# A two-layer diffusion backbone in fp32: first layer's values split in high and low side by side, normalising on GpSimd, stage memory shared

## Chip, core and metric

One NeuronCore of a Trainium2 chip runs the whole program. The metric is the device time in microseconds of one launch. Kernel before: median 2120.17 us of 3 runs (2116.49 to 2120.89).

## The reference, cut

Tokens: 1024 latent ones on a 16 x 64 grid and 256 context ones, width 1024, fp32. Two layers, each: a modulation from a condition vector, one input projection to queries, keys, values and gate, a mixer, gating by SiLU, an output projection, a residual sum and a layer norm.

```python
h = x * (1.0 + sc) + sh
q, k, v, z = jnp.split(h @ w_in[l], 4, axis=-1)
# layer 0: 16 heads of 64, window of 8 x 16 grid cells plus all context keys, bias by relative position
s = jnp.concatenate([s_loc.reshape(b, h, GRID_W, n_win), s_ctx], axis=-1)
p = jax.nn.softmax(s, axis=-1)
y = p_loc @ v_win + p_ctx @ vc
# layer 1: 8 heads, difference of two softmax maps over all 1280 keys, rotary embedding, RMS norm per head
out = (y * jax.nn.silu(z)) @ w_out[l]
x_new = _layer_norm(DEEPNORM_ALPHA * x + (1.0 + g) * out, ln_g[l], ln_b[l])
```

Context queries of layer 0 attend to context keys alone. Layer 1 has no context output.

## The kernel before

The program is written engine by engine, in blocks: each engine has a queue of its own whose order is the order of the code, and semaphores tie the queues together. No planner reorders anything. A block ends when all engines have ended it. Blocks: `modulation` (layer 0's shift and scale, by matmul); `neighbourhood` (layer 0: tokens turned, modulated and split, then the chunks); `differential` (first `Project` of layer 0 and tokens of layer 1, then its chunks); `Project` of layer 1.

**Split products.** A fast matmul format (fp32r) holds fewer bits, so projections and scores split each operand in a high part (a rounding copy) and a low part (the difference), and sum the products. The projection does high x high, high x low, low x high (L528). Values (L1079) and transposes (L1065) are plain fp32.

**A chunk** is 128 of the 1024 columns: two heads of layer 0, or one of layer 1. `each_chunk` loops over 8, the last one written out apart. Within a chunk of layer 0: weight blocks come in the order value, key, query, gate, each for token groups of 512, 512 and 256 columns (12 products j). Four products of the next chunk (values, first keys) are pieces put between attention work (`fill`). `pe_part` turns the values by transposes (`turn_v`, L540), which open the chunk, then runs products 4 to 9.

**An item** is one head and one block of 128 queries: 16 local items (384 window keys + 256 context keys = 640 columns, five blocks of 128) and 4 context items (256 columns). Each goes: `scores` on TensorE (L1051 context, L1055 local, high and low keys), bias sum (L979) and negated row maximum (L981) on DVE, exponential with row sum on ScalarE (L933), reciprocal (L986) and normalising (L989) on DVE, transposes in batches of 3 and 2 blocks (L1065), a copy to SBUF on ScalarE (L940), value matmuls (L1079), gating straight from PSUM on DVE (L1002). Items are two apart in each queue. DVE also makes a quarter-row of layer 1's modulation per chunk (`LateModulation.sum`, L344), splits weights (`split_lo_part`, L497), and splits keys (`split_k`, L682, L686) and queries (`split_q`, L705, L709) from SBUF copies that ScalarE made (L582).

**Bias tables.** `Bias.expand` on GpSimd writes tables in DRAM: 32 DMAs from the table of relative positions (L270), a wait for all, 8 DMAs to a form by query (L277). `biases[0]` holds the first chunk's 2 heads and is expanded in the modulation block; `biases[1]` holds the other 14 and is expanded in the first layer's block, after the tokens are turned and a memset of the tables' frame in SBUF (L905). SP loads the tables of the next chunk with 48 DMAs in a chunk (L863), one head at a time; it waits for the expansion before the first of them, and weights and late rows queue behind it.

**Memory.** `Memory` holds arrays for the whole program; `big`, `aux`, `pt` and `extra_prob` are used by several stages for different things.

Of the kernel before, what the change touches and what calls it, by code (L numbers as in the profile page):

```python
# [19 lines left out]
P = 128  # L20
D = 1024
SEQ = 1024
# [47 lines left out]
CREDIT = 1  # L70
ROW_PAD = P
AHEAD = 4

# [6 lines left out]
class Memory:  # L80


    def __init__(self, nc, stack):
# [10 lines left out]
        self.v = sb("v", [P, TOK_TILES, P])  # L94
# [3 lines left out]
        self.big = sb("big", [P, 5120])  # L98
        self.aux = sb("aux", [P, 4608])
        self.extra_prob = sb("extra_prob", [P, TOK])  # L100
        self.pt = sb("pt", [P, 4, 4 * P])
# [20 lines left out]
def na_values(m, i):  # L122

    if i < 8:
        return m.big[:, 2560 + i * P:2560 + (i + 1) * P]
    return m.v[:, i - 8, :]


def na_values_from(m, i, n):

    first = na_values(m, i)
    return bass.AP(first.tensor, first.offset, [list(first.ap[0]), [1, n]])
# [8 lines left out]
def modulation(nc, m, stack, w_mod, cond_in, b_cols_in, lam_in, sub_in, ident_in, biases, load_tile, load_weights):  # L141
# [4 lines left out]
            [b[:, 0:D] for b in (m.k_raw, m.gate, m.y)] + [m.v[:, 0:KT, :].rearrange("p k n -> p (k n)")]  # L146
# [8 lines left out]
    row_buf = [m.pt[0:2, i, :] for i in range(4)]  # L155
    lam = m.extra_prob[:, 0:4 * HD]
    lam_prod = m.extra_prob[:, 4 * HD:5 * HD]
    sums = m.stats[:, 0:4]

    with nc.Block() as block:  # L160
        @block.sync
        def _(sp):
# [15 lines left out]
            sp.wait_ge(turned, 1)  # L178
# [69 lines left out]
class Bias:  # L248
# [14 lines left out]
    def expand(self, pool):  # L263
        n = len(self.heads)
        for rows in range(2):
            for cols in range(2):
                for c in range(STRIP):
                    src = self.rpb[rows, cols, self.heads[0], :, STRIP - 1 - c:2 * STRIP - 1 - c]
                    dst = self.by_column[rows, c, cols * NEAR:(cols + 1) * NEAR].rearrange("s h d j -> s (h d) j")
                    pool.dma_start(dst, bass.AP(src.tensor, src.offset, [[STRIP, NEAR], [RPB_W, n * RPB_H], [1, STRIP]]))\  # L270
                        .then_inc(self.columns_out, 16)
        pool.wait_ge(self.columns_out, 16 * 4 * STRIP)
        for rows in range(2):
            for r in range(BAND):
                src = self.by_column[rows, :, :, :, BAND - 1 - r:BAND - 1 - r + K_ROWS, :]
                dst = self.by_query[rows, r * STRIP:(r + 1) * STRIP]
                pool.dma_start(dst.rearrange("c s h n -> c (s h) n"), src.rearrange("c s h d j -> c (s h) (d j)"))\  # L277
# [6 lines left out]
def bias_parts():  # L284

    parts = []
    for b in range(ROW_BLOCKS):
        for half in range(2):
# [3 lines left out]
            for s in range(2):  # L292
                for kind in range(KINDS):
# [4 lines left out]
                    parts.append((half * 64 + s * CELL, b, at, high - low + 1, first - K_BAND0[b], last - first + 1,  # L298
                                  rows, cols * NEAR + low - strip + 1, first - band + 1))
# [3 lines left out]
class LateModulation:  # L303

    AHEAD = 3

    def __init__(self, nc, m, stack, w_mod, mod_rows):
# [1383 lines left out]
```

## Time and profile before

| | us |
|---|---|
| median of 3 runs | 2120.17 |
| the profiled execution | 2119.15 |
| its span | 2117.3 |
| TensorE busy | 1913.3 (90%) |
| VectorE busy | 1297.0 (61%) |
| ScalarE busy | 890.6 (42%) |
| GpSimd busy | 148.0 (7%) |
| granted TensorE clock, mean | 0.965 |

Busy time is the time in which an engine has an instruction under way; matmuls overlap each other, so a start-to-start distance says more of TensorE's cost than a duration does. A line number is that of the kernel before. In a row of a group, after the count stand the busy sum in us, the mean of one in ns, and the idle time before them with what ended it. In a row of the timeline the first two numbers are start and duration in us, and brackets hold the idle time before it and its releaser.

### The profile page before, as it was taken

How to read it: one execution, taken by the hardware profiler on the slowest of the kernel's cores; microseconds unless marked ns; L12 is line 12 of the kernel's file. 1: busy time of each engine (PE TensorE's matmuls, PEld its weight loads, DVE VectorE, ACT ScalarE, POOL GpSimd, SP SyncE). 2: the span in 40 equal slices, each digit the busy share in tenths (PEclk: the TensorE clock that was granted, in tenths of full speed). 3: DMA queues.
4: the chain of work that ended last, by engine and by line, in shares of the span. 5: the costliest groups of instructions: out<-in, count | busy, mean ns of one | idle time of the engine just before them, and what ended most of it. 6: DMA issues, size and time to landing. Idle time of an engine off the chain costs nothing. (4 is left out here: it accounts for less than half of the span.)

```text
span 2117.3 us, 31607 instructions
## 1 busy us (share of the span) xinstructions
PE 1913.3 (90%) x11121; PEld 1629.3 (77%) x11121; DVE 1297.0 (61%) x2074; ACT 890.6 (42%) x1560; POOL 148.0 (7%) x155
## 2 busy tenths in 40 slices
PE   6879799999999999968989999999999989998697
PEld 2768687978888888856867878787887878787576
DVE  1557384747474757585875566565747474747567
ACT  0434253535354444451134536463636363635410
POOL 4234000000000000001100000000000000000000
PEclk9899899999999999998999999999999999999899
DMA  8476422222222222125411010101000000001142
GB/s 272 67 59 49 110 62 55 62 54 64 58 61 56 63 54 65 44 91 179 149 70 40 11 40 10 40 10 38 12 30 20 30 20 23 16 20 40 55 175 100
DMA packets 137392, 130.80 MB, mean 62 GB/s; under 512 B 46672, under 2 KB 112560, under 8 KB 137216
## 3 DMA queue, kind: packets, MB, share of 16 engines
q1 hardware_dynamic: 125008, 98.22, 16.3%
q0 software_dynamic: 9744, 22.51, 6.0%
q10 hardware_dynamic: 2592, 9.44, 1.1%
q8 instruction: 29, 0.48, 0.1%
q14 instruction: 19, 0.16, 0.0%
HBM read 110.81 MB, written 22.00 MB: 63 GB/s over the span
## 5 line engine op out<-in xcount | busy, mean ns | idle before, releaser
L528 PE MATMUL acc<-h_hi,w_hi 128*128 128x512 f32 (+1 forms) x1408 | 524.7, 373 | 14.6 <-DVE w_lo L497 5.0
L528 PE MATMUL acc<-h_lo,w_hi 128*128 128x512 f32 (+1 forms) x1408 | 512.4, 364 | 0.0
L528 PE MATMUL acc<-h_hi,w_lo 128*128 128x512 f32 (+1 forms) x1408 | 512.3, 364 | 0.0
L528 PEld LDWEIGHTS acc<-h_hi,w_hi 128*128 128x128 f32 x1408 | 269.4, 191 | 55.6 <-issue 15.8
L528 PEld LDWEIGHTS acc<-h_hi,w_lo 128*128 128x128 f32 x1408 | 268.6, 191 | 42.4
L528 PEld LDWEIGHTS acc<-h_lo,w_hi 128*128 128x128 f32 x1408 | 269.6, 191 | 33.6
L1367 PE MATMUL acc<-k_dup,q_stack 128*128 128x512 f32 (+1 forms) x768 | 192.3, 393 | 38.2 <-DVE q_stack L709 24.5
L1281 DVE TENSOR_REDUCE stats<-acc 128x1 f32<-128x1280 f32 x128 | 190.3, 1487 | 53.0 <-PE acc L1367 52.9
L940 ACT ACTIVATE pt<-acc 128x256 f32<-128x256 f32 (+1 forms) x288 | 123.4, 432 | 203.5 <-PE acc L1065 203.3
L1367 PEld LDWEIGHTS acc<-k_dup,q_stack 128*128 128x128 f32 x768 | 145.9, 205 | 79.6 <-issue 24.4
L1388 PE MATMUL acc<-pt,v 128*128 128x128 f32 x1280 | 175.0, 277 | 0.8
L1220 ACT ACTIVATE pt<-acc 128x512 f32<-128x512 f32 (+1 forms) x192 | 100.8, 525 | 155.4 <-PE acc L1376 152.6
L1388 PEld LDWEIGHTS acc<-pt,v 128*128 128x128 f32 x1280 | 160.6, 193 | 3.0 <-issue 1.9
L1079 PE MATMUL acc<-pt,v 128*128 128x128 f32 x1024 | 159.4, 276 | 0.6 <-DVE y L1002 0.6
L1213 ACT ACTIVATE big<-acc,stats 128x1280 f32<-128x1280 f32 x96 | 127.5, 1329 | 76.0 <-DVE stats L1281 74.2
L1065 PE MATMUL acc<-ident,big 128*128 128x128 f32 x704 | 125.5, 277 | 35.5 <-DVE big L989 35.5
L1079 PEld LDWEIGHTS acc<-pt,v 128*128 128x128 f32 x1024 | 136.9, 192 | 2.5 <-issue 1.9
L1065 PEld LDWEIGHTS acc<-ident,big 128*128 128x128 f32 x704 | 85.8, 141 | 58.5 <-issue 23.0
L497 DVE TENSOR_TENSOR w_lo<-w_raw,w_hi 128x1024 fp32r<-128x1024 f32 x64 | 78.4, 1224 | 80.9 <-ACT w_hi L492 79.7
L933 ACT ACTIVATE big<-acc,stats 128x640 f32<-128x640 f32 (+1 forms) x160 | 116.5, 728 | 26.1 <-DVE stats L981 26.0
L1376 PE MATMUL acc<-ident,big 128*128 128x128 f32 x640 | 103.9, 277 | 24.0 <-DVE big L1294 23.4
L1574 PE MATMUL acc<-h_hi,w_hi 128*128 128x512 f32 x288 | 91.8, 400 | 25.5 <-DVE w_lo L1514 25.4
(189 smaller groups left out, 2725.1 us busy)
## 6 DMA issues: line engine op xcount, KB each, us to landing
w_raw<-in_w_in SPq DMA_DIRECT2D x64, 512.0 KB, 4.1
extra_prob<-in_w_mod SPq DMA_DIRECT2D x40, 256.0 KB, 2.8
w_raw<-y_t POOLq DMA_DIRECT2D x18, 512.0 KB, 5.6
w_raw<-in_w_out SPq DMA_DIRECT2D x16, 512.0 KB, 3.3
big<-in_w_mod SPq DMA_DIRECT2D x24, 256.0 KB, 2.8
y_t<-y SPq DMA_DIRECT2D x8, 640.0 KB, 3.4
y_t<-y SPq DMA_DIRECT2D x8, 512.0 KB, 2.8
big<-x POOLq DMA_DIRECT2D x8, 512.0 KB, 3.7
```

The source lines that it names most:

```text
L528: mm = nc.tensor.matmul(m.bank(self.bank_of(j), w), wt[:, b % 2, k, :], ht[:, k, t0:t0 + w], start=(k == 0 and i == 0), stop=(k == KT - 1 ...
L933: nc.scalar.activation(prob[:, i % PB, 0:it.width], all_scores(i), ACT.Exp, bias=stat(i, 2), accum_out=stat(i, 3)).then_inc(exp_done, 1)
L940: nc.scalar.activation(m.pt[:, n % 3, 0:w], m.bank(4 + n % 2, w), ACT.Copy).then_inc(pt_ready, 1)
L1065: mm = nc.tensor.transpose(m.psum[:, 4 + n % 2, t * P:(t + 1) * P], prob[:, i % PB, (a + t) * P:(a + t + 1) * P], m.ident[:, :])
L1079: mm = nc.tensor.matmul(m.psum[:, 6, (it.n % 4) * P:(it.n % 4 + 1) * P], na_values(m, it.blocks[a + t]), m.pt[:, n % 3, t * P:(t + 1) * P] ...
L1213: nc.scalar.activation(prob(mp, t), m.banks(3 * mp, 0, TOK), ACT.Exp, bias=stat(t, mp), accum_out=stat(t, 2 + mp)).then_inc(exp_done, 1)
L1220: nc.scalar.activation(m.pt[:, n % 4, 0:w], m.bank(6, w), ACT.Copy).then_inc(pt_ready, 1)
L1281: nc.vector.reduce_max(stat(t, mp), m.banks(3 * mp, 0, TOK), AX, negate=True).then_inc(max_done, 1)
L1367: mm = nc.tensor.matmul(m.bank(3 * mp + g, w), m.q_stack[:, mp, t * P:(t + 1) * P], m.k_dup[:, mp, part, k0:k0 + w], start=(part == 0), st ...
L1376: mm = nc.tensor.transpose(m.psum[:, 6, i * P:(i + 1) * P], prob(0, t)[:, (a + i) * P:(a + i + 1) * P], m.ident[:, :])
L1388: mm = nc.tensor.matmul(m.psum[:, 7, (t % 4) * P:(t % 4 + 1) * P], m.v[:, a + i, :], m.pt[:, n % 4, i * P:(i + 1) * P], start=(a + i == 0) ...
L1574: mm = nc.tensor.matmul(m.bank(2 * (i % 3) + half), yt[:, i % 2, k, :], wt[:, k, half * 512:half * 512 + 512], start=(k == 0 and n == 0), ...
```

## The change

Layer 0's attention is rewritten, layer 1's only renamed; arrays are placed stage by stage at shared addresses.

- Items go in pairs, a `Unit`: one head, two blocks of queries (both row blocks of a column block). 10 units in a chunk. TensorE's queue has a unit's scores, then the transposes of the unit before in batches of 3, 4 and 3 blocks (context: 4), value matmuls two batches behind, and products of the next chunk at two places of a step.
- Values are kept split, high and low side by side: 64 + 64 columns as one stationary operand, with 256 queries moving. ScalarE writes the high half of the turned probabilities (`take_hi`), DVE the low half (`take_lo`). The result has two halves, summed by `take_low` (ScalarE) and `sum_y` (DVE), then `gate_y`.
- Keys and queries are split straight from PSUM (`split_x_hi` on ScalarE, `split_x_lo` on DVE).
- Normalising goes to GpSimd, as a multiply with a factor of step 0; `biases[1]` is expanded ahead of it in the same queue, without waiting for the tokens. The memset of the tables' frame goes to the modulation block.
- Tables are loaded by kind of column block (3 kinds, 16 DMAs each). Late rows have two slots in place of three.
- The scratch for GpSimd's DMA descriptors is set to 4096 bytes. The call before named no size (the library's default is 16384).

```diff
-    def expand(self, pool):
+    def expand_columns(self, engine):
...
+    def expand_queries(self, engine):
+        engine.wait_ge(self.columns_out, 16 * 4 * STRIP)
...
             def _(pool):
...
-            biases[0].expand(pool)
+            biases[0].expand_columns(pool)
+            biases[0].expand_queries(pool)
+            nc.gpsimd.memset(near.bias[:, :], NEG).then_inc(near.bias_set, 1)
...
+class Unit:
...
+            self.batches = [(1, 0, [(0, 1), (1, 0), (0, 0)], [band(1), band(0)]),
+                            (2, 0, [(0, 2), (1, 1), (0, 3), (1, 3)], [band(2), ctx[0]]),
+                            (0, P, [(1, 2), (0, 4), (1, 4)], [band(3), ctx[1]])]
+        else:
+            self.width = CTX
+            self.batches = [(2, 0, [(0, 0), (1, 0), (0, 1), (1, 1)], ctx)]
...
             @block.gpsimd
             def _(pool):
-                pool.wait_ge(tokens.turned, 3 * KT)
-                nc.gpsimd.memset(m.aux[:, :], NEG).then_inc(bias_set, 1)
-                biases[1].expand(pool)
+                biases[1].expand_columns(pool)
+                biases[1].expand_queries(pool)
+
+                def chunk(c, last):
+                    def normalise(i):
+                        pool.wait_ge(recip_done, CREDIT + c * NI + (i + 1))
+                        factor = stat(i, 4)
+                        factor = bass.AP(factor.tensor, factor.offset, [list(factor.ap[0]), [0, units[i // 2].width]])
+                        nc.gpsimd.tensor_tensor(probs(i), probs(i), factor, ALU.mult).then_inc(p_ready, 1)
...
+                    p.act_part(act, c, lambda e: e.wait_ge(y_ready, CREDIT + c * COLS), last)
+                    for step in range(NU + 1):
+                        old = of_unit[step - 1] if step else []
+                        for n in old[:1]:
+                            take_hi(n)
+                        if step < NU:
+                            exp(2 * step)
+                        for n in old[1:2]:
+                            take_hi(n)
+                        if step % 2 and step >= 3:
+                            take_low(step // 2 - 1)
+                        if step < NU:
+                            exp(2 * step + 1)
+                        for n in old[2:]:
+                            take_hi(n)
...
+                        if step < NU:
+                            row_max(2 * step)
+                        for n in old[:1]:
+                            take_lo(n)
+                        if step < NU:
+                            row_max(2 * step + 1)
+                        for n in old[1:2]:
+                            take_lo(n)
+                        if step < NU:
+                            reciprocal(2 * step)
+                        if step % 2 and step >= 3:
+                            sum_y(step // 2 - 1)
+                        if step < NU:
+                            reciprocal(2 * step + 1)
+                        for n in old[2:]:
+                            take_lo(n)
+                        if step % 2 and step >= 3:
+                            gate_y(step // 2 - 1)
...
+                    def turn(n):
+                        s, j, slot, first, tiles, blocks = batches[n]
+                        pe.wait_ge(p_ready, CREDIT + c * NI + 2 * s + 2)
...
+                        for t, block in enumerate(blocks):
+                            for pt in (near.pt_hi, near.pt_lo):
+                                mm = nc.tensor.matmul(m.psum[:, 6, u.head * 2 * P:(u.head + 1) * 2 * P],
+                                                      near.values[:, block, u.head, :], pt[:, slot, t * 2 * P:(t + 1) * 2 * P],
...
+                    for step in range(NU + 1):
+                        if step < NU:
+                            scores(step)
+                        for position, n in enumerate(of_unit[step - 1] if step else []):
+                            turn(n)
+                            if n >= 2 and step < NU:
+                                values(n - 2)
+                            if step == NU - 1:
+                                values(n - 1)
+                            if position == 1:
+                                fill_in(step, MIDDLE)
...
-    nc = bacc.Bacc("TRN2", target_bir_lowering=False, num_devices=1)
+    nc = bacc.Bacc("TRN2", target_bir_lowering=False, num_devices=1, dynamic_dma_scratch_size=4096)
```

## Rows read from the trace of the kernel before

**Rows 1.** The page's first part: busy us, share of the span, instructions.
```profile
PE 1913.3 (90%) x11121; PEld 1629.3 (77%) x11121; DVE 1297.0 (61%) x2074; ACT 890.6 (42%) x1560; POOL 148.0 (7%) x155
```
**Rows 2.** Timeline of TensorE: the first transposes of chunks 0, 1, 2, 4, 5, 7.
```profile
93.27 1.03 PE L540 MATMUL acc<-ident,k_raw 128*128 128x128 f32 x8
...
212.99 1.03 PE L540 MATMUL acc<-ident,k_raw 128*128 128x128 f32 x8
...
329.25 1.03 PE L540 MATMUL acc<-ident,k_raw 128*128 128x128 f32 x8
...
537.32 1.03 PE L540 MATMUL acc<-ident,k_raw 128*128 128x128 f32 x8
...
641.37 1.04 PE L540 MATMUL acc<-ident,k_raw 128*128 128x128 f32 x8
...
849.48 1.03 PE L540 MATMUL acc<-ident,k_raw 128*128 128x128 f32 x8
```
**Rows 3.** Windows of chunk 4: projection, then attention; busy us (instructions), clock, DMA.
```profile
537.32:566.85 29.53, 29.53 (x163) 25.60 (x162) 12.15 (x18) 11.15 (x15) 0.00 (x0) 1.00 0.21 60
566.85:641.37 74.52, 70.56 (x485) 62.83 (x485) 53.01 (x104) 36.07 (x86) 0.00 (x0) 1.00 0.23 59
```
**Rows 4.** Timeline of GpSimd, 0 to 220 us.
```profile
6.87 20.72 POOL L270 DMA_DIRECT2D first_by_column<-in_rpb  x32
...
78.00 3.94 POOL L905 MEMSET aux<- 128x4608 f32 x1 [40.24 <-PE acc L397]
81.88 5.61 POOL L270 DMA_DIRECT2D rest_by_column<-in_rpb  x4
97.62 5.58 POOL L270 DMA_DIRECT2D rest_by_column<-in_rpb  x4 [10.14 <-issue]
...
206.41 5.28 POOL L277 DMA_DIRECT2D rest_by_query<-rest_by_column  x8 [10.27 <-DMA rest_by_column<-in_rpb]
```
**Rows 5.** Timeline of TensorE in chunk 4: projection of 256 columns, values.
```profile
558.98 0.28 PE L528 MATMUL acc<-h_lo,w_hi 128*128 128x256 f32 x1
559.10 0.28 PE L528 MATMUL acc<-h_hi,w_lo 128*128 128x256 f32 x1
...
585.58 0.61 PE L1079 MATMUL acc<-pt,big 128*128 128x128 f32 x4
```
**Rows 6.** Groups by line with shapes kept apart, whole span.
```profile
L1079 PE MATMUL acc<-pt,v 128*128 128x128 f32 x1024 | 159.4, 276 | 0.6 <-DVE y L1002 0.6
...
L1079 PE MATMUL acc<-pt,big 128*128 128x128 f32 x384 | 64.2, 276 | 0.4 <-DVE y L1002 0.3
...
L709 DVE TENSOR_TENSOR q_stack<-y,q_stack 64x512 fp32r<-64x512 f32 x64 | 43.9, 686 | 2.0
...
L671 POOL TENSOR_TENSOR big<-big,aux 128x512 f32<-128x512 f32 x32 | 41.4, 1293 | 820.4 <-DVE big L660 820.4
```
**Rows 7.** Timeline of chunk 4's attention, 611 to 613 us.
```profile
611.21 0.55 DVE L989 TENSOR_SCALAR big<-big,stats 128x640 f32<-128x640 f32 x1
...
611.89 0.54 PE L1065 MATMUL acc<-ident,big 128*128 128x128 f32 x3 [1.44 <-DVE big L989]
612.01 0.55 DVE L979 TENSOR_TENSOR acc<-acc,aux 128x384 f32<-128x384 f32 x1
...
612.47 0.49 ACT L940 ACTIVATE pt<-acc 128x384 f32<-128x384 f32 x1 [1.85 <-PE acc L1065]
612.60 0.82 DVE L981 TENSOR_REDUCE stats<-acc 128x1 f32<-128x640 f32 x1
```
**Rows 8.** Timeline of SP: the last chunk's result is stored.
```profile
949.37 0.35 SPq L889 DMA_DIRECT2D y_t<-y  x1
```
**Rows 9.** L270 issues at 81.9, at 84.7 and 86.1, at 112.2: time to landing.
```profile
DMA to landing us min/median/max: 8.0/8.0/8.0
...
DMA to landing us min/median/max: 10.2/10.7/11.2
...
DMA to landing us min/median/max: 5.8/5.8/5.8
```

More of the change, by code:

```diff
@@ L70 @@
 CREDIT = 1
+AHEAD = 4
 ROW_PAD = P
-AHEAD = 4
 def f(ap):
@@ L806, in neighbourhood @@
-    late = LateModulation(nc, m, stack, w_mod, mod_rows)
+    turned, pt_hi, pt_ready, av_done = sem("turned"), sem("pt_hi"), sem("pt_ready"), sem("av_done")
+    y_low, y_sum, y_ready, y_stored = sem("y_low"), sem("y_sum"), sem("y_ready"), sem("y_stored")
+    late = LateModulation(nc, m, near, stack, w_mod, mod_rows)
     counters += late.counters
-    items = [Item(h, n) for h in range(2) for n in range(TOK_TILES)]
-    NI = len(items)
-    NL = sum(it.local for it in items)
-    WMAX = LOCAL + CTX
@@ L823, in neighbourhood @@
-    NT = len(turns)
-    YG = 6
-    last_item = [max(i for i, it in enumerate(items) if it.y_group == g) for g in range(YG)]
-    local_before = [sum(x.local for x in items[:i]) for i in range(NI + 1)]
-    BL = 16 * 2 * len(bias_parts())
-    assert NI % 2 == 0 and NT % 6 == 0 and NI % PB == 0
-    z0, z1, z2 = p.gate_groups
-    fill = {-1: (0, z1, 0, 4), 0: (0, z1, 4, 8), 2: (0, z2, 0, 4), 3: (0, z2, 4, 8)}
-    for i, k in ((4, 0), (5, 2), (6, 4), (7, 6), (8, 7)):
-        fill[i] = (1, 0, k, min(k + 2, 7) if i < 8 else 8)
@@ L834, in neighbourhood @@
-    for i in range(4):
-        fill[9 + i] = (1, 1, 2 * i, 2 * i + 2)
-        fill[13 + i] = (1, 2, 2 * i, 2 * i + 2)
-        fill[17 + i] = (1, 3, 2 * i, 2 * i + 2)
-    filled = {i: (next_chunk, j) for i, (next_chunk, j, k0, k1) in fill.items() if k1 == KT}
+    units = [Unit(s) for s in range(2 * (COL_BLOCKS + 1))]
+    NU = len(units)
+    NI = 2 * NU
+    NL = sum(2 * u.local for u in units)
+    bias = near.bias[:, :].rearrange("p (h b s n) -> p h b s n", h=2, b=ROW_BLOCKS, s=KINDS * K_STRIPS)
@@ new lines, in bias_of @@
+    def bias_of(u, row):
+        s0 = u.kind * K_STRIPS
+        return bias[:, u.head, row, s0:s0 + K_STRIPS, :].rearrange("p s (g n) -> p g s n", n=CELL)
+    batches = [(s, j) + b for s, u in enumerate(units) for j, b in enumerate(u.batches)]
+    NT = len(batches)
+    of_unit = [[n for n, b in enumerate(batches) if b[0] == s] for s in range(NU)]
+    slot_free = [max([i + 1 for i in range(n) if batches[i][2] == b[2]], default=0) for n, b in enumerate(batches)]
+    local_before = [2 * sum(x.local for x in units[:i // 2]) + i % 2 for i in range(NI)]
@@ L840, in stat @@
+    filled = {step: piece[0:2] for (step, half), piece in fill.items() if piece[3] == KT}
     def stat(i, col):
@@ L892, in _ @@
+                sp.wait_ge(tokens.turned, 3 * KT)
                 for u in range(late.AHEAD):
                     late.load(sp, 0, u)
[L894 to L897 removed]
                 each_chunk(sp, chunk)
@@ new lines, in chunk @@
+                    for step in range(NU + 1):
[12 more added lines that the diff above has]
+                            take_hi(n)
+                        take_filled(step)
+                        if step == 3 and not last:
@@ L1123, in _, with differential @@
+                    if last:
+                        pe.wait_ge(p.gate_done, CREDIT + c * p.q_groups + 3)
+                    else:
+                        pe.wait_ge(p.evac, CREDIT + (c + 1) * p.evacs + 3)
+                    values(NT - 2)
+                    late.reduce(pe, c)
+                    values(NT - 1)
                 each_chunk(pe, chunk)
     return counters, run
-def differential(nc, m, stack, p, tokens, before, out_w, rope_in, y_out):
+def differential(nc, m, far, stack, p, tokens, before, out_w, rope_in, y_out):
```

854 lines of the change are left out of this document (462 added, 392 removed).

## The prediction

> **What bounds the kernel now.** I read the page first: TensorE is busy 90% of the span and no other engine more than 61% [rows 1]. So TensorE's queue is followed next, by stage. The program has a short start (modulation, then tokens), eight chunks of layer one, a join, eight chunks of layer two and an end; the change touches the first two. The transposes that open a chunk (turn_v, L540) date the chunks: chunk 0 begins at 93.27, then 212.99, 329.25, and so on at 537.32, 641.37 and, for the last, 849.48 [rows 2]. A steady chunk takes 641.37 - 537.32 = 104.05 us; chunk 0 took 119.7, chunk 1 116.3, together 27.9 above two steady ones. The table by stage splits a steady chunk in 29.5 us of projection, in which TensorE never rests, and 74.5 of attention, with 70.56 busy and 3.96 idle [rows 3]. GpSimd does nothing in either. Layer one is bound by TensorE's work, and what lies on GpSimd is free. In chunks 0 and 1 it isn't: GpSimd's queue there works on the bias tables until about 212 [rows 4], and the excess of 27.9 us hangs on DMA and on tables that come late.
>
> **TensorE's part.** Value matmuls in plain fp32 cost two instructions each: four in a row from 585.58 fill 0.61 us where one lasts 0.275, so they start (0.61 - 0.275) / 3 = 0.112 us apart [rows 5, 6]. The groups count (1024 + 384) / 8 = 176 in a chunk, 19.7 us [rows 6]. The new form joins two query blocks: a local unit (two items) has 6 value blocks x high and low = 12 matmuls of 256 columns, a context unit 4, so 8 x 12 + 2 x 4 = 104. Split projection matmuls of 256 columns follow each other by 559.10 - 558.98 = 0.12 us [rows 5], so 12.5 us. That takes 7.2 us from each chunk, 58 us in all, if TensorE stays the bound. The 88 transposes and the scores stay as many.
>
> **The splits.** Keys and queries are split straight from PSUM. DVE's 12.15 us of the projection stage [rows 3] are this splitting, but for one weight split of 1.2: about 10.7 us go, and 8 subtractions of 64x512 (0.69 us [rows 6]) and 4 of half the width (0.42 by proportion and a fixed part) come, 7.2. It gains 10 subtractions for low values (0.42 or less, 3.9), the low halves of turned probabilities (0.55 for 384 columns, priced by the sum of that width [rows 7], 0.69 for 512; 15.9 in all) and 2.7 in the new sum and gating, and loses 16 x 0.55 + 1.4 = 10.2 of normalising [rows 7]. That is 65 + 9 = 74 us in a chunk: no bound as a sum. In the projection stage ScalarE and DVE have 11 and 12 us of 29.5 [rows 3]; DVE gets 11 more and five sums of the late modulation (1.4 each), so it fills 25 to 29 of 29.5. I cost it at nothing; the cover is TensorE's 29.5 us. The duplication of the keys lies under the last two products too.
>
> **Normalising on GpSimd.** One item has 640 columns; GpSimd's multiply of 512 took 1.292 us [rows 6], so 1.6 us (1.4 to 1.8; a stride-0 factor may cost or save), where DVE took 0.55 [rows 7]. By itself hidden, it now lies in a chain, since the order written out makes each step need the one before. In step s TensorE turns unit s-1, whose two items must both be normalised. From that turn: ScalarE's copy begins 0.52 to 0.58 later (611.89 to 612.47) and takes 0.49, the low half 0.55, then the second row maximum (bias sum 0.59 from 612.01 to 612.60, maximum 0.82) [rows 7]: 2.5 to 3.1 us, I take 3.05. From there DVE still subtracts the second batch (0.69) and takes the first reciprocal (0.19) before GpSimd may start: GpSimd is then behind both, 2 x 1.61 in a row, and TensorE starts 0.13 after it [rows 6, 7] (the turn at 611.89 after the normalising from 611.21 to 611.76). With some 0.1 of handing over: 3.05 + 0.69 + 0.19 + 3.22 + 0.25 = 7.4 us a step. TensorE's own work in steps 2 to 5 is scores 1.19, transposes 1.08, values 1.44 and pieces of the next projection 2.72 = 6.4 us. So the chain, not TensorE, sets the steps.
>
> The attention stage, from its start: first turn at 8.0 (gating of the first group 1.65, two maxima 2.8, reciprocal, two multiplies), second at 16.1 (a gating pushes in), five steps of 7.4 to 53.1, 0.3 for the weight split in step 3, one more to 60.8, then two short context steps (5.7, 4.5) and 3.5 for the last values and the reduction of the late row: 74.5 us. That is the present 74.5 [rows 3]. The 7.2 us saved turn into waiting: a steady chunk stays at 104 (between 97, TensorE alone, and 109). The last chunk has no products of a next one as filler, so it was at 99.9 us to its store (949.37, [rows 8]) against 104.05 + 1.5 of a steady one; the chain makes it 106 to 109: +8 us.
>
> A rule that speaks against the change stands in the Trainium skill, SBUF — State Buffer, "Who interferes with whom": a DVE instruction with two SBUF inputs and a GpSimd instruction that reads SBUF exclude each other, the later one waits to the end. No row before shows both at once. It is rival (4) below, which is priced without it.
>
> **GpSimd's queue at the start.** This decides the sign. The tables of the other 14 heads are expanded by 32 + 8 DMAs on GpSimd; before they end it can't normalise anything. In the kernel before they start at 81.88 and the last eight at 206.41 + 5.28 [rows 4]: 130 us that hid behind nothing but SP's wait. After the change the wait for the tokens is gone, so they start at the block's start, 48 us; TensorE wants the first normalised unit at about 130 to 137.
>
> Their pace changes too. They come four at a time (5.6 us), then a pause until the fourth has landed: issue 86.1 + 11.2 = 97.3, next at 97.62 [rows 4, 9]. The first tables, with a seventh of the data, went 32 in a row with no pause, 20.72 us [rows 4]. So what is limited is not the number of DMAs but of pieces: by the code 630 runs in one large DMA, 90 in a small one; 2880 pass, 5 x 630 = 3150 don't. The change sets the descriptor memory to 4096 bytes where the library's default is 16384: a quarter, 720 to 787 runs, one large DMA at a time. The first of a burst lands 5.8 us (in the second listed) to 8.0 after its issue [rows 9]; I take 6.15 and 0.3 to the next, 32 x 6.45 = 206 us, bounded by 130 (no effect of the size) and 266 (8.0 each). The last eight: 5.3 of issue, two pauses: 12.5.
>
> The same limit splits the first tables in five bursts, four pauses of 5.4 minus some overlap; the queue ends the modulation stage with a memset of 3.9 us [rows 4] at about 61 instead of before the others are done (48): +13 (0 to 20). Addresses shared between stages add no wait of their own: the blocks' ends already order the stages, and late rows, which now wait for the tokens to be turned, are first summed in chunk 0, behind its 29.5 us of projection.
>
> **The sum.** Expansion ends 61 + 206 + 12.5 = 279.5; two multiplies and a turn: 283. Attention after the first turn 66.5: chunk 1 starts at 349.5, chunk 2 at 453.5 with no excess left, since tables and weights are now early. It was at 329.25 [rows 2]: +124. Chunks 2 to 6: 0. Last chunk: +8. Join and layer two: 0, their products and order are the same, and the second x tile is only fetched earlier beside TensorE. The profiled execution took 2119.15 us, span 2117.3, 1.0 below the median of 2120.17. 2119 + 124 + 8 = 2251; I say 2250.
>
> **Rivals.** (1) The size of the descriptor memory does nothing. Expansion runs 48 to 178, first turn 181.5, chunk 2 at 350.5: +21, with the last chunk +8: 2148. For it: the pause may have another cause; against it: small and large DMAs differ just by pieces. (2) Other side: besides (1), the chain is shorter than TensorE's work (multiplies below 1.2 us, or handed over earlier), chunks of 97: chunk 2 at 339, six times -7, last chunk +2: 2119 + 10 - 35 + 2 = 2096, faster. It decides once a step's chain is below 6.4 us and the tables end before about 190. For it: 7.2 us less TensorE work is sure; against: reciprocal after second maximum is written into the order. (3) Two large DMAs fit at once, 4.4 us each: 140 us, 2185. (4) GpSimd's multiply, 28 us of a chunk now, and DVE hold each other up in memory, or the landings take 8.0 each: four DVE pieces a chunk, each late by up to one multiply of 1.6 us on the chain, are 3 to 5 us, 24 to 40 in all, or 60 more at the start: 2280 to 2310. No row before has both engines on SBUF at once, so nothing speaks for or against it but that the pieces stand in the chain. (5) The new pieces do not overlap as written (projection stage runs over by DVE): +1 to 3 us a chunk, 2265.
>
> **Chances.** The forecast together with (5) 0.50, (4) 0.13, (3) 0.08, (1) 0.16, (2) 0.11, something else faster 0.02. The predicted time is the likeliest case, 2250. Leaving out (2) and the top of (4), the range is 2130 to 2290. Some 0.2% (4 us) is what a measurement tells from no change: faster 0.13, same 0.02, slower 0.85.
>
> **What would show it.** Right: GpSimd's row is full from 61 to about 280 with one table DMA every 6 to 7 us; TensorE idles some 140 us in chunk 0, released by GpSimd's multiply; L540's successors lie 104 us apart; TensorE's busy sum falls by about 55. In a step, the turn waits for the second multiply. Wrong: bursts of four as before (then 2150), TensorE without waits in steps 2 to 5 (then chunks of 97), multiplies far from 1.6 us, a second layer that moves by more than 3 us.

## The result, and the profile after

| | median of the runs, us | runs, us | profiled span, us | ratio, 95% interval |
|---|---|---|---|---|
| before | 2118.33 | 2111.96 to 2120.89 | 2117.3 | |
| after | 2214.97 | 2212.61 to 2218.07 | 2210.8 | 1.046, 1.043 to 1.049 |

The change makes the kernel 4.6% slower, 97 us. The forecast was 2250, with a range of 2130 to 2290.

The first part of the page of after answers to [rows 1]; busy us, share of the span, instructions:

```profile
PE 1857.1 (84%) x10545; PEld 1573.4 (71%) x10545; DVE 1375.2 (62%) x2246; ACT 935.6 (42%) x1648; POOL 325.9 (15%) x315
```

TensorE's work fell by 1913.3 - 1857.1 = 56.2 us, as the wider value matmuls promise, and yet its share fell from 90% to 84%: it waits more than it did. Where, the starts of the chunks tell, as in [rows 2] (timeline of TensorE, chunks 0, 2, 4 and 8 of sixteen; the last line is SyncE's store of the last result of layer one, as in [rows 8]; x8 and x2 only say how many transposes a line lumps together):

```profile
102.76 1.03 PE L534 MATMUL acc<-ident,k_raw 128*128 128x128 f32 x8
...
431.89 0.38 PE L534 MATMUL acc<-ident,k_raw 128*128 128x128 f32 x2
...
634.53 1.03 PE L534 MATMUL acc<-ident,k_raw 128*128 128x128 f32 x8
...
1216.78 1.03 PE L534 MATMUL acc<-ident,k_raw 128*128 128x128 f32 x8
...
1047.59 0.35 SPq L1028 DMA_DIRECT2D y_t<-y  x1
```

Chunk 2 starts 431.89 - 329.25 = 102.6 us later than before. From there a chunk takes 101.32 us where it took 104.05, so chunk 7 starts at 938.46, and five chunks have given back 13.7. The last chunk takes 1047.59 - 938.46 = 109.1 to its store instead of 99.9: +9.2. The join is 1.1 longer, layer two 5.8 shorter. The sum: 102.6 - 13.7 + 9.2 + 1.1 - 5.8 = 93.4, and the spans differ by 93.5.

GpSimd's timeline says where the 102.6 come from, answering to [rows 4], and TensorE's first turn of normalised probabilities stands behind it:

```profile
61.52 1.42 POOL L313 DMA_DIRECT2D rest_by_column<-in_rpb  x1 [1.55 <-POOLq L201]
67.36 1.43 POOL L313 DMA_DIRECT2D rest_by_column<-in_rpb  x1 [4.43 <-issue]
...
247.96 1.40 POOL L313 DMA_DIRECT2D rest_by_column<-in_rpb  x1 [4.38 <-issue]
253.72 3.34 POOL L322 DMA_DIRECT2D rest_by_query<-rest_by_column  x5 [4.36 <-DMA rest_by_column<-in_rpb]
...
263.53 2.47 POOL L1053 TENSOR_TENSOR near_prob<-near_prob,stats 128x640 f32<-128x640 f32 x2
266.05 1.33 PE L1246 MATMUL acc<-ident,near_prob 128*128 128x128 f32 x5 [125.74 <-POOL near_prob L1053]
```

The 32 large table DMAs go one at a time, (247.96 - 61.52) / 31 = 6.0 us apart (5.76 where nothing disturbs them), and the first multiply of chunk 0 stands behind all of them. TensorE waits 125.74 us in one piece. Its granted clock is at its lower level, 0.50, from 143.7 to 270.0 us, so chunk 0 pays a little for that too, in the first 4 us after the wait.

Inside a steady chunk, the windows of chunk 4 (projection, attention) answer to [rows 3], and the list of what TensorE waited for in it follows (us in total, times, longest):

```profile
634.53:664.50 29.97, 29.97 (x167) 26.07 (x166) 21.55 (x38) 17.43 (x31) 0.00 (x0) 1.00 0.34 100
664.50:735.85 71.35, 63.80 (x412) 55.72 (x411) 54.08 (x104) 35.35 (x82) 22.24 (x20) 1.00 0.18 45
```
```profile
PE acc L1261 <- DVE y L1166: 3.5, 3, 1.6
PE acc L1246 <- POOL near_prob L1053: 3.5, 4, 0.9
PE acc L1246 <- DVE near_pt_lo L1158: 0.4, 1, 0.4
```

The projection stage is still TensorE's alone: VectorE's 21.55 us lie under its 29.97. In the attention stage TensorE has 6.8 us less to do than in [rows 3], and it idles 7.55 where it idled 3.96. Half of that is the multiplies' chain (L1053). The other half was in nobody's sum: values (L1261) wait for VectorE's sum_y (L1166), which frees the bank of the result (the part of PSUM that holds it) for the next column.

### The profile page after: what moved, and what is told of

It is laid out like the page before. It is cut to its first block and busy times, and to the rows that moved or that the text cites. A ratio compares the mean times of both kernels' runs of the same rounds, so it can differ in the third digit from the quotient of the medians.

```text
span 2210.8 us, 30825 instructions
## 1 busy us (share of the span) xinstructions
PE 1857.1 (84%) x10545; PEld 1573.4 (71%) x10545; DVE 1375.2 (62%) x2246; ACT 935.6 (42%) x1648; POOL 325.9 (15%) x315
## 5 line engine op out<-in xcount | busy, mean ns | idle before, releaser
L1053 POOL TENSOR_TENSOR near_prob<-near_prob,stats 128x640 f32<-128x640 f32 (+1 forms) x160 | 177.9, 1131 | 597.7 <-DVE stats L1154 597.6
L1246 PE MATMUL acc<-ident,near_prob 128*128 128x128 f32 x704 | 116.0, 283 | 164.1 <-POOL near_prob L1053 157.9
L1158 DVE TENSOR_TENSOR near_pt_lo<-acc,near_pt_hi 128x384 fp32r<-128x384 f32 (+1 forms) x208 | 125.6, 604 | 175.6 <-ACT near_pt_hi L1092 174.4
L1092 ACT ACTIVATE near_pt_hi<-acc 128x384 fp32r<-128x384 f32 (+1 forms) x208 | 109.7, 528 | 273.5 <-PE acc L1246 231.8
L1392 ACT ACTIVATE far_prob<-acc,stats 128x1280 f32<-128x1280 f32 x128 | 169.9, 1328 | 72.2 <-DVE stats L1460 69.6
L1568 PE MATMUL acc<-far_pt,far_v 128*128 128x128 f32 x1280 | 175.6, 278 | 0.6
L1568 PEld LDWEIGHTS acc<-far_pt,far_v 128*128 128x128 f32 x1280 | 161.2, 194 | 3.2 <-issue 2.1
L1261 PE MATMUL acc<-near_pt_hi,near_values 128*128 128x256 f32 x416 | 126.9, 327 | 31.3 <-DVE y L1166 31.3
L1086 ACT ACTIVATE near_prob<-acc,stats 128x640 f32<-128x640 f32 (+1 forms) x160 | 116.8, 730 | 70.1 <-DVE stats L1150 60.7
L1555 PE MATMUL acc<-ident,far_prob 128*128 128x128 f32 x640 | 104.3, 278 | 25.7 <-DVE far_prob L1473 23.9
```

What stands on the lines that cost most here:

```text
L1053: nc.gpsimd.tensor_tensor(probs(i), probs(i), factor, ALU.mult).then_inc(p_ready, 1)
L1086: nc.scalar.activation(probs(i), all_scores(i), ACT.Exp, bias=stat(i, 2), accum_out=stat(i, 3))\
L1092: nc.scalar.activation(turned_part(near.pt_hi, n), turned_bank(n), ACT.Copy).then_inc(pt_hi, 1)
L1158: nc.vector.tensor_tensor(turned_part(near.pt_lo, n), turned_bank(n), f(turned_part(near.pt_hi, n)), ALU.subtract).then_inc(pt_ready, 1)
L1246: mm = nc.tensor.transpose(m.psum[:, 4 + n % 2, first + t * P:first + (t + 1) * P], probs(2 * s + row)[:, a * P:(a + 1) * P], m.ident[:, :])
L1261: mm = nc.tensor.matmul(m.psum[:, 6, u.head * 2 * P:(u.head + 1) * 2 * P], near.values[:, block, u.head, :], pt[:, slot, t * 2 * P:(t + 1) ...
```

## The experiments

Each ran beside the kernel before; medians are given, and chunk lengths come from the traces. The numbers of a trace belong to one execution, whose total can lie some us from the median.

**1. The descriptor memory alone.** In the kernel before, `Bacc(..., num_devices=1)` becomes:

```diff
-    nc = bacc.Bacc("TRN2", target_bir_lowering=False, num_devices=1)
+    nc = bacc.Bacc("TRN2", target_bir_lowering=False, num_devices=1, dynamic_dma_scratch_size=4096)
```

> The kernel before with one number changed: 4096 bytes of descriptor memory instead of the default. Theory (the size sets how many pieces may be under way): the 32 large table DMAs of the other heads go one at a time, 5.8 to 6.5 us apart, instead of four in 11.2 us; the first 32 small ones get pauses; the tables end at about 280 instead of 212, so chunk 1's attention (its place is 242 us) waits some 40 us more for them, and the run is 40 to 65 us longer: about 2170. Steady chunks stay at 104.05. Rival (the size does nothing, the pace after comes from something else in the change): bursts of four as before, 2118 within 4 us.

Measured 2199.9 against 2118.1: ratio 1.039 (1.036 to 1.041), 82 us for one number. GpSimd's timeline of this run:

```profile
17.61 5.18 POOL L270 DMA_DIRECT2D first_by_column<-in_rpb  x8 [5.49 <-issue]
...
105.18 1.41 POOL L270 DMA_DIRECT2D rest_by_column<-in_rpb  x1 [4.40 <-issue]
...
277.10 1.40 POOL L270 DMA_DIRECT2D rest_by_column<-in_rpb  x1 [4.34 <-issue]
282.83 3.33 POOL L277 DMA_DIRECT2D rest_by_query<-rest_by_column  x5 [4.33 <-DMA rest_by_column<-in_rpb]
```

A run is here one contiguous stretch of elements that a DMA moves, the prediction's piece. Small tables go in bursts of eight (8 x 90 runs = 720), large ones (630 runs) one at a time: it is the number of runs under way that is limited, and the limit follows the size. Chunk 0 took 104.0 us, chunk 1 203.5. The loss is larger than the 40 to 65 I gave, since I let only the bias loads wait. SyncE's wait for the tables also stands ahead of a weight load of the next projection, and TensorE waited 84.8 us for that (L497), in chunk 1. Steady chunks stayed at 104.1. The reverse, the changed kernel with the default size, was not run: its arrays leave no room in SBUF for it.

**2. GpSimd's queue freed at the start.** In the changed kernel the 32 large tables are issued by ScalarE at the end of the modulation stage, the 8 that follow by SyncE (the second hunk stands in SyncE's block, the third in GpSimd's):

```diff
+            act.wait_ge(piece_used, 12)
+            biases[1].expand_columns(act)
...
+                biases[1].expand_queries(sp)
...
-                biases[1].expand_columns(pool)
-                biases[1].expand_queries(pool)
```

> The changed kernel with the 32 large table DMAs issued by ScalarE and the 8 that follow by SyncE, so that GpSimd's queue is free for normalising in chunk 0. Theory: chunk 0 has no wait for GpSimd; chunks 1 and 2 start about 101 us apart (at 204 to 208 and 305 to 310 instead of 330.6 and 431.9), all else stays, so 2215 - 122 = 2093, between 2080 and 2105, faster than before (2118). Rival (the chain through GpSimd's multiply was most of the loss): 2150 or more, with chunks above 104.

Measured 2154.8, ratio 1.018 (1.015 to 1.021): the chunks are those of the theory, the total lies where the rival has it. Chunks now follow each other in 102.3, 101.3, 101.3 us, so no chunk waits for GpSimd; but chunk 0 starts at 171.0, since the issuing itself is long, and TensorE stands for the end of the block that ScalarE is the last to reach:

```profile
63.01 9.79 ACTq L315 DMA_DIRECT2D rest_by_column<-in_rpb  x4
...
130.55 4.91 PE L426 MATMUL acc<-ident,token_rows 128*128 128x128 f32 x28 [82.99 <-PEq L201]
...
131.67 1.63 ACT L436 ACTIVATE token_tmp<-acc,mod_cols 128x512 f32<-128x512 f32 x2 [118.78 <-PE acc L426]
```

An issue of 630 runs holds ScalarE's queue for 9.79 / 4 = 2.45 us, against 1.40 on GpSimd and 0.4 for a plain weight load. The mechanism was confirmed, but of the 125.5 us that chunk 0 gets shorter (227.8 to 102.3), the later start (171.0 instead of 102.8) takes 68 back.

**3. Normalising back on VectorE**, GpSimd keeps only the tables (its loop of multiplies goes):

```diff
                         nc.vector.reciprocal(stat(i, 4), stat(i, 3)).then_inc(recip_done, 1)
+                        v.wait_ge(recip_done, CREDIT + c * NI + (i + 1))
+                        nc.vector.tensor_scalar(probs(i), probs(i), stat(i, 4), None, ALU.mult).then_inc(p_ready, 1)
```

> The changed kernel with normalising back on VectorE, where the kernel before has it; GpSimd keeps the tables. Theory (a step's chain is set by two multiplies of GpSimd in a row): chunks become as long as TensorE's work, about 97.5 us instead of 101.3; chunk 0 does not wait, but chunk 1 waits for tables that end at about 261, some 30 to 36 us; chunk 2 starts at about 336; in all about 2080 (2065 to 2095). Rival (VectorE's sum, then some 84 us a chunk, binds instead): chunks of 101 or more, 2110 or more.

Measured 2188.6, ratio 1.034 (1.031 to 1.036): the theory missed twice. Steady chunks take 102.0 to 103.3, not 97.5: VectorE is at 81.4 us of 102, and TensorE waits 5.9 us for sum_y. The window of one:

```profile
606.71:708.67 101.96, 94.67 (x576) 82.99 (x575) 81.39 (x162) 53.11 (x112) 0.00 (x0) 0.98 0.23 60
```

TensorE idles 7.29 us in it, where it idles 7.55 in the same chunk of the changed kernel. The 0.6 us by which this chunk is longer are TensorE's busy time (94.67 against 93.77) at a granted clock of 0.98 instead of 1.00, so moving the multiply changed what TensorE waits for, and hardly how long. And the start still loses 98 us, by another road:

```profile
PE acc L390 <- DVE near_late_acc L383: 97.3, 1, 97.3
```
```profile
SPq L1016 <- DMA rest_by_query<-rest_by_column: 135.4, 1, 135.4
```

SyncE waits for the tables, behind it stand the last loads of the late modulation, VectorE waits for these, and TensorE for VectorE's last sum. So tables whose last DMA is issued at 263 us cost 98 us in chunk 0 with VectorE normalising (200.3 against 102.0) and 126 with GpSimd (227.8 against 101.3). Moving normalising to GpSimd adds 28 of them; the rest comes from the pace of the tables, which has two ways of reaching TensorE.

**4. The first reciprocal earlier**, ahead of the second low half:

```diff
                         if step < NU:
                             row_max(2 * step + 1)
+                            reciprocal(2 * step)
                         for n in old[1:2]:
                             take_lo(n)
-                        if step < NU:
-                            reciprocal(2 * step)
```

> The changed kernel with the first reciprocal of a step ahead of the second batch's low half on VectorE; nothing else. Theory (chain through copy, low half, second maximum, 0.69 low half, reciprocal, two multiplies): GpSimd's first multiply starts 0.7 us earlier and leaves the path; steps of about 6.4 instead of 6.9, 2 to 4 us a chunk, 2215 - 16 to - 32: about 2190. Rival (steps are held elsewhere: the bank of the result freed late by VectorE's sums, or the gating that waits for GpSimd): less than 1 us a chunk, above 2207.

Measured 2199.4, 15.6 us below the changed kernel; chunks of 99.45 (-1.9). TensorE's waits in a steady chunk:

```profile
PE acc L1260 <- DVE y L1166: 3.5, 3, 1.6
PE acc L1245 <- POOL near_prob L1053: 1.7, 4, 0.7
```

The wait for the multiplies halves, the one for the bank doesn't move. The chain stands at the place that the prediction gave it; the gain lies just below the 2 to 4 us a chunk that I gave, and the wait for the bank (3.5 us) is the largest that is left.

**5. Column sums and gating at the beginning of an odd step**, added to 4 (their old places, behind the low halves, are emptied):

```diff
+                        if step % 2 and step >= 3:
+                            take_low(step // 2 - 1)          # ScalarE, ahead of take_hi
...
+                        if step % 2 and step >= 3:
+                            sum_y(step // 2 - 1)             # VectorE, ahead of row_max
+                            gate_y(step // 2 - 1)
```

> The changed kernel with the reciprocal of the run above ahead of the second low half, and with ScalarE's copies of a finished column, VectorE's sums and the gating moved from the middle and end of an odd step to its beginning, where both engines wait for TensorE (2.7 and 1.2 us). Theory (of the 7.6 us that TensorE waits in a steady chunk 3.5 are for the bank of the result, freed by these sums, 3.5 for the multiplies): both waits nearly go, chunks of 96.5 to 98 us, in all 2199 - 8 x 2.5 = 2179 (2170 to 2186). Gating takes 0.42 us, since no multiply of GpSimd runs beside it. Rival (the early sums only push the row maxima back and the chain grows by what the bank saves): chunks of 99 or more, 2195 or more.

Measured 2296.8: 97 us slower than 4, chunks of 112.7. I had misread TensorE's order. It runs the values two batches late, so the last two batches of a column are multiplied inside the odd step, behind the turns of the next unit. The idle time at its beginning can't be used, for the result isn't there:

```profile
764.89 0.78 ACT L1100 ACTIVATE y<-acc 64x256 f32<-64x256 f32 x2 [3.41 <-PE acc L1259]
```

ScalarE and VectorE stand there with the exponentials and row maxima of the next unit behind them. Part of the loss is the clock. A chunk of this run:

```profile
678.17:790.86 112.69, 98.55 (x576) 84.99 (x575) 73.76 (x142) 52.88 (x112) 22.64 (x20) 0.95 0.20 55
```

Of the 13.2 us over a chunk of 4 (99.45, with 93.77 of TensorE's work at a clock of 1.00), 8.5 are waiting and 4.8 slower work: TensorE waits four times for 2.8 to 3.5 us, and at the end of three of these waits the granted clock falls to 0.50 for 3.4 us.

**6. Gating beside the multiply.** As 5, but with gate_y left at the end of the step:

```diff
                             sum_y(step // 2 - 1)
-                            gate_y(step // 2 - 1)
...
+                        if step % 2 and step >= 3:
+                            gate_y(step // 2 - 1)
```

> The kernel of the run above, but with the gating (product of two SBUF operands on VectorE) left at the end of the step, where GpSimd's second multiply runs. Theory (VectorE's instruction with two SBUF inputs and GpSimd's multiply exclude each other): gating takes 1.1 to 1.35 us, from its start to about 0.3 us after the multiply's end, in four of five columns, and 0.40 in the last, with no multiply beside it; a chunk is up to 1 us longer than in the run above. Rival (the long gating of the changed kernel has another reason, such as the layout of its operands): the same duration in both places.

Measured 2285.2. Total and chunks (109.5 to 112.9) are ruled by the mistake of 5 and say nothing; the duration does. In 5 all 40 gatings took 424 to 427 ns. Here they take 0.40 to 0.43 us or 1.09 us (three of five in a chunk the long one, not the four that I expected), by what GpSimd does meanwhile:

```profile
652.53 2.47 POOL L1053 TENSOR_TENSOR near_prob<-near_prob,stats 128x640 f32<-128x640 f32 x2 [7.19 <-DVE stats L1154]
...
654.18 1.09 DVE L1171 TENSOR_TENSOR y<-y,gate 128x256 f32<-128x256 f32 x1
...
675.93 0.42 DVE L1171 TENSOR_TENSOR y<-y,gate 128x256 f32<-128x256 f32 x1
```

The multiplies end at 655.00, the gating at 655.27; the one at 675.93 has none beside it. All 24 that start beside a multiply of 640 columns end 0.28 us after it. So the gating, which came second, waits for the multiply's end; the multiplies keep their 1.25 us.

**7. The tables shared between the queues**, in the changed kernel. SyncE's loads of biases[0] kinds 1 and 2 also move behind its first late rows:

```diff
-                biases[1].expand_columns(pool)
-                biases[1].expand_queries(pool)
+                biases[1].expand_columns(pool, 0, 12)
...
+                biases[1].expand_columns(sp, 12, 14)     # SyncE, behind load_bias kind 0
+                biases[1].expand_columns(sp, 14, 20)     # behind the third weight load
...
                         p.load_next(sp, c, (6,))
+                        if first:
+                            biases[1].expand_columns(sp, 20, 32)
+                            biases[1].expand_queries(sp, 12)
```

> The changed kernel with the 32 large table DMAs shared: 12 on GpSimd before its first multiply (they end at about 132), 8 on SyncE between its first loads, 12 and the 8 that follow on SyncE inside chunk 0, where it waits; the loop of SyncE has chunk 0 written out. By the last such run an issue takes 2.5 us on a hardware queue. Theory (the loss at the start is GpSimd's queue alone): chunk 0 starts at 103 as before this edit and lasts 101 to 108, so the run is 2215 - 120 to - 126 = 2092 (2085 to 2102). Rival (the pieces of the tables hold up the loads of weights and tokens, as ScalarE's issues did): chunk 0 starts after 110 or lasts over 115, 2110 or more.

Measured 2092.1 (2091.5 to 2092.9), ratio 0.987 (0.985 to 0.988): 123 us below the changed kernel, and 1.3% below the kernel before. SyncE's issues, GpSimd's first multiply, and the starts of chunks 1 and 2:

```profile
129.31 31.12 SPq L317 DMA_DIRECT2D rest_by_column<-in_rpb  x12
...
138.27 2.47 POOL L1068 TENSOR_TENSOR near_prob<-near_prob,stats 128x640 f32<-128x640 f32 x2
...
207.48 1.03 PE L539 MATMUL acc<-ident,k_raw 128*128 128x128 f32 x8
...
308.77 1.03 PE L539 MATMUL acc<-ident,k_raw 128*128 128x128 f32 x8
```

Chunk 0 starts at 100.0 and takes 107.5, all others 101.3. All but some 6 us of the loss at the start was the queue of tables. The edit frees GpSimd's road and SyncE's together and doesn't part them.

**8. Edits 4, 5 and 7 together**, their diffs unchanged:

> The three edits together (reciprocal earlier, column sums early, tables shared). If they act in different places they add up: 2215 - 123 - 36 = 2056 (2045 to 2070), 3% below the kernel before. If the earlier sums and the shared tables press on the same thing in chunk 0, above 2075.

Measured 2174.5, ratio 1.025 (1.023 to 1.027), again with chunks of 112.7. The 36 us that I counted for the other two edits rested on 5, whose result I hadn't seen. Against run 9 below, the early sums cost 96.6 us, as they did between 4 and 5 (97.4): edits add up, bad ones too.

**9. Edits 4 and 7**, their diffs unchanged:

> The changed kernel with the tables shared between the queues and the reciprocal earlier, the column sums where they were. The two edits gave 122 and 15 us alone, in different places: 2215 - 122 - 15 = 2077 (2072 to 2082), 2% below the kernel before, chunks of 99.5 us. The rival, that they press on each other in chunk 0, gives up to 2090.

Measured 2077.9, ratio 0.981 (0.979 to 0.983); chunks 107.3, then 99.4.

**10. The second multiply on VectorE**, added to 9 (the even items keep GpSimd):

```diff
+                        if i % 2:
+                            v.wait_ge(recip_done, CREDIT + c * NI + (i + 1))
+                            nc.vector.tensor_scalar(probs(i), probs(i), stat(i, 4), None, ALU.mult).then_inc(p_ready, 1)
```

> The run above, with the second item of each unit normalised by VectorE (0.4 to 0.55 us), the first by GpSimd. Theory (the second multiply of 1.25 us still ends the chain of a step): TensorE's waits for normalising, 1.7 us a chunk, go; chunks of 98 to 99. Rival (VectorE has no room left in a step, as with all normalising on it, 102 us): chunks of 100 or more.

Chunks take 98.1 us and the wait for GpSimd is gone, as the theory has it. The total stays: 2077.1, ratio 0.979 (0.976 to 0.982). Layer one ends 5.1 us earlier in this trace than in that of 9 (last store at 904.2 against 909.3), but layer two, whose code is the same, is 10.3 us longer: its chunks took 110.3 and 111.4 in turn instead of 108.6 and 109.9. The trace of 9 is of its fastest execution, so the two traces differ by more than the medians do. More on layer two below.

**11. The filler first**, added to 9: the piece of the next projection that stood at the end of steps 3, 5 and 7 moves to their middle, ahead of the turn whose values wait for the bank:

```diff
+    for step in (3, 5, 7):
+        next_chunk, j, k0, k1 = fill[step, MIDDLE]
+        fill[step, MIDDLE] = (next_chunk, j, k0, fill.pop((step, END))[3])
```

> The run before the last, with the whole piece of the next projection moved to the middle of steps 3, 5 and 7, ahead of the turn after which TensorE waits for the bank of the result (3.5 us a chunk). Theory: that wait is covered, of 3.5 us some 2 are gained, chunks of 97.5 to 98.5. Rival (the turn comes 1.4 us later, and with it the low halves and the next step): chunks of 99.5 or more.

Measured 2065.0 (2063.8 to 2066.0), ratio 0.974 (0.971 to 0.977), the best of all. Chunks take 97.0 us with 93.6 of TensorE's work; the waits:

```profile
PE acc L1263 <- POOL near_prob L1071: 2.0, 5, 0.7
PE acc L1278 <- DVE y L1184: 0.9, 1, 0.9
```

The same bank, the same sums at the same place: only what TensorE does meanwhile has changed.

**12. What the old form gets from the same cure.** In the kernel before, 15 large tables and the 8 that follow go to SyncE, between its loads of chunk 0, and 17 stay:

```diff
-                biases[1].expand(pool)
+                biases[1].expand_columns(pool, 0, 17)
...
                         late.load(sp, c, u)
+                        if first:
+                            at = 17 + 3 * (u - late.AHEAD)
+                            biases[1].expand_columns(sp, at, at + 3)
...
+                        if first:
+                            biases[1].expand_queries(sp, 17)
                         biases[1].wait(sp)
```

> The kernel before, nothing changed but the large table DMAs: 17 stay on GpSimd, 15 go to SyncE between its loads of chunk 0 (2.5 us an issue), and the 8 that follow too. It asks how much of the gain of the shared tables the old form would have had as well. Theory (chunks 0 and 1 last 119.7 and 116.3 us for tables and loads that come late, not for their own work): they shorten to 104 to 108 each, in all 2118 - 18 to - 27, about 2097, and the steady chunks stay at 104.05. Rival (the tables hold up other loads): no gain, 2115 or more.

Measured 2102.8, ratio 0.993 (0.992 to 0.995), a little less gain than the 18 to 27 us expected. Chunk 1 falls from 116.3 to 104.0, chunk 0 only from 119.7 to 115.7. With the start mended in both, the new form stands at 2092.1 against 2102.8 for the old, and at 2065.0 with its two edits of order. Run 11 is 55 us below the kernel before that ran beside it, run 12 is 17 below its own. So 17 of the 55 come from the tables alone and 38 from the new form and its order, if the two cures of the start, which share out the tables differently, are worth the same.

## Why the forecast came out right, step by step

- **Descriptor memory, one large table at a time: right**, by 1. The pace was 6.0 us, not 6.45: undisturbed issues follow each other in 5.76, which is the 5.8 of [rows 9], not the 6.15 and 0.3 that I took between it and the 8.0. The 32 tables ended at 253.7, not 267, and the last eight took 9.8 instead of 12.5. They began at 61.5, given as 61, though the small tables went in four bursts and not five.
- **Normalising waits for the tables: right** in the changed kernel (125.7 us of waiting, given as some 140). But 3 shows that there were two roads, and that the other one alone costs 98 us. I priced the new road and took the old one, SyncE's wait, for harmless, since it had cost little when tables ended at 212.
- **TensorE's part: right.** Its busy time was to fall by 58 us (7.2 a chunk), and by the page 56.2 go.
- **Hidden in the projection stage: right.** It takes 29.97 us instead of 29.53, TensorE never idle; VectorE has 21.55 us there, given as 25 to 29. Rival (5) didn't come.
- **The chain of a step: place right, term too large.** In chunk 4 the first multiplies of the eight local units follow each other by 7.7, 6.3, 6.5, 9.6, 6.3, 7.6 and 6.3 us, 50.4 in all (the long one holds a weight split and 8.4 us of TensorE's work). The prediction has 60.8 - 8.0 = 52.8 for the same seven. The mis-sized term is the multiply: 1.25 us for 640 columns where I had 1.61, so 0.72 less for two. I scaled the 1.29 us of 512 columns from [rows 6] by width, but that one reads two whole operands. The new one reads a single value per row for its factor:

```profile
L1053 POOL TENSOR_TENSOR near_prob<-near_prob,stats 128x640 f32<-128x640 f32 x128 | 157.8, 1254 | 529.6 <-DVE stats L1154 529.5
...
L1053 POOL TENSOR_TENSOR near_prob<-near_prob,stats 128x256 f32<-128x256 f32 x32 | 20.1, 638 | 68.1 <-DVE stats L1154 68.1
```

  By these two, a column costs (1254 - 638) / 384 = 1.60 ns, and by estimate 512 of them would take 1.05 us. The row that would have bounded this wasn't there; I named a stride-0 factor as a doubt and still kept 1.4 as the lower end.
- **A term missing: the bank of the result.** 52.8 less 7 x 0.72 would give 47.8, and the seven took 50.4. Two of them, those of 9.6 and 7.6 us, hold a wait of TensorE for sum_y (0.94 and 0.96 us), and a third one of 1.62 comes in the next. It matters as much as the wait for the multiplies (3.5 us a chunk each), and 11 shows that order alone cures most of it. I had sum_y in VectorE's sum only, not among what TensorE waits for.
- **Steady chunk: 104 forecast, 101.32 measured**, so six chunks gave back 2.7 each.
- **Last chunk +8: right**, 109.1 to the store, given as 106 to 109.
- **Layer two 0: it gave 5.8**, while its code is the same; its chunks go with the clock (below), so this part of the distance from the forecast is luck.
- **Rival (4), the memory ports.** The mechanism was real, but the 24 to 40 us that I gave it didn't come: steady chunks are shorter than forecast. The Trainium skill, SBUF — State Buffer, "Who interferes with whom", says that a VectorE instruction with two SBUF inputs and a GpSimd instruction that reads SBUF keep each other out for the whole instruction. The traces agree: 0.42 us alone, 1.09 to 1.35 beside a multiply. In the changed kernel it hits three gatings a chunk, some 2.8 us of VectorE's time. A sum of the late modulation (L383), also with two inputs in SBUF, takes 0.74 us alone and 1.10 where it starts at 731.63 beside a multiply. How much of this reaches TensorE I can't say, since run 6 can't tell. Instructions that read PSUM with one of their inputs take beside a multiply what they take alone (0.55 and 0.56 for the low half of 384 columns).
- **Rival (2), chunks of 97 and a faster kernel**, was three edits away (7, 4 and the filler of 11). It asked for tables that end before about 190, and in run 11 SyncE issues the last of them by 172; it asked for a chain shorter than TensorE's work, and its chunks are 97.0. The run gave 2065.
- **Two slips in the rivals' sums.** Rival (1) puts chunk 2 at 350.5; by the terms of the forecast it is 181.5 + 66.5 + 104 = 352, which makes 2150. Rival (2) says six times -7 and subtracts 35: from chunk 2 to chunk 7 there are five.

The sum of the deviations: chunk 1 came 18.9 us early (17 by the tables, 2 by its attention, 64.5 us after the first turn instead of 66.5), six chunks 2.7 shorter (16), the last and the join 2 longer, layer two 5.8 shorter: 2251 - 18.9 - 16 + 2 - 5.8 = 2212, beside 2212.6 of the profiled execution.

## What to carry to other kernels

When work moves to an engine, read first what is already queued on it in program order, and then at what pace that queue will run in the new kernel: here a memory size cost 82 us by itself, and its effect reached TensorE by two roads. A saving on the bounding engine is only worth what the next chain lets through. Write down every semaphore on which that engine waits in a step, for banks as well as for data, and put its filler work ahead of the longest, before touching the engines that it waits for. Before moving work into an idle gap, look at whether its input exists by then, in the order of the engine that makes it. Before reading a chunk that came out a microsecond longer as a longer wait, compare the bounding engine's busy time and its granted clock in the two windows.

## What the hardware showed beyond that

- **Issuing many short runs costs the issuing queue**: 630 runs take 2.45 us of ScalarE's queue in run 2, 31.12 / 12 = 2.6 of SyncE's in run 7, and 1.40 of GpSimd's. While the first loads of weights and tokens were running, the first three on ScalarE took 22.1 us together, and in run 12, where two or three stand between other loads, the first of each row took 0.7 to 0.9. "Another queue" isn't free.
- **Layer two's chunks come in three lengths**, about 108.6, 110 and 111.3 us, with the same instructions. They go with the granted clock. Two chunks of the changed kernel, then one of the kernel before:

```profile
1436.79:1545.39 108.60, 101.96 (x608) 87.97 (x607) 67.05 (x97) 54.86 (x82) 5.17 (x4) 1.00 0.08 24
1545.39:1655.26 109.87, 103.22 (x608) 89.03 (x606) 67.16 (x97) 54.90 (x82) 5.17 (x4) 0.98 0.08 24
```
```profile
1448.94:1560.13 111.19, 104.49 (x608) 90.04 (x607) 67.22 (x97) 54.93 (x82) 5.17 (x4) 0.97 0.08 24
```

  In the second of these the clock stands at its lower level once, and at 1.00 in the rest:

```profile
1573.91:1577.33 3.42, 2.92 (x8) 2.46 (x9) 2.58 (x4) 0.36 (x1) 0.00 (x0) 0.50 0.07 17
```

  The chunk of 111.19 has one such stretch of twice the length, 1476.9 to 1483.8. In the 28.5 us ahead of the stretch that is shown TensorE was busy for 25.95; what sets it off wasn't found. Which length comes changes between runs and also within one: the kernel of run 1, whose layer two is that of before, has chunks of all three. So differences of 5 to 10 us in a total can be the clock's. Run 10 is the case in point: its chunks of layer one are sure to be shorter, its total isn't.
